# A hybrid decoder layer: state update of the sample sequences in pairs, gate sums on array quarters, a replayed DMA model in the scheduler, Ln and Exp for two roots, and another memory layout

## What is computed

```python
z = a @ w_in                       # q | k | v | r | alow (16 columns) | u | vg
log_a = log_sigmoid(alow @ w_a2 + b_a) / 16     # decay of each key channel
# gated linear attention, token by token:
S = exp(log_a_t) * S + k_t^T v_t ;  o_t = q_t S
o = rmsnorm(o) * silu(r)
m = rmsnorm(gelu(u) * (W_s @ layernorm(gelu(vg)) + b_s))
h = h + concat(o, m) @ w_out ;  h = h + swiglu_ffn(rmsnorm(h))
h = h + rmsnorm(p @ w_ple) * sigmoid(rmsnorm(h) @ w_ple_gate)
```

## Time and profile before

| | |
|---|---|
| median of 3 runs | 1830.63 us (1829.62 to 1832.37) |
| the profiled execution | 1828.47 us |
| its span, slowest core (5) | 1827.2 us |
| spans of the 8 cores | 1819.9 to 1827.2 us |
| mean granted TensorE clock of the cores | 0.991 to 0.996 |
| busy in core 5 | PE 97%, DVE 43%, ACT 29%, POOL 8% |

### The profile page before, as it was taken

One profiled execution on the slowest core, in us unless ns is written; L12 is line 12 of the kernel. 1 busy time (PEld: TensorE's weight loads), 2 busy tenths in 40 slices (PEclk: granted clock), 3 DMA queues, 4 the chain that ended last, 5 costly groups with the idle time before them and its releaser, 6 DMA issues.

```text
span 1827.2 us, 26969 instructions; the slowest of 8 cores (1819.9 to 1827.2 us)
## 1 busy us (share of the span) xinstructions
PE 1774.8 (97%) x10012; PEld 945.1 (52%) x10012; DVE 788.9 (43%) x1232; ACT 522.4 (29%) x932; POOL 142.0 (8%) x139
## 2 busy tenths in 40 slices
PE   4899999999999999999999999999999999999996
PEld 2465545544544566555555555555656565644443
DVE  6565524634533520242424151515151515167886
ACT  4854525655611320000000000000000000017886
POOL 1001212222000000000000000000000000000000
PEclk9899999999999999999999999999999999999998
DMA  9951486065575272424242433334242433376332
GB/s 259 229 128 60 137 199 148 2 116 109 150 145 110 41 127 47 93 47 93 47 84 55 74 66 66 74 57 83 48 90 48 82 58 71 71 146 121 87 100 79
DMA packets 57272, 175.59 MB, mean 96 GB/s; under 512 B 17972, under 2 KB 19380, under 8 KB 53304
## 3 DMA queue, kind: packets, MB, share of 16 engines
q0 software_dynamic: 28960, 108.60, 33.2%
q1 hardware_dynamic: 27896, 64.74, 10.7%
q10 hardware_dynamic: 288, 0.52, 0.1%
HBM read 259.90 MB, written 18.87 MB: 153 GB/s over the span
## 4 chain that ended last, share of the span: by engine, by line
PE 93%; DMA 2%; DVE 2%; ACT 1%; issue 1%; SPq 0%; ACTq 0%; DVEq 0%
PE pf L510 92%; DMA arena<-xp 2%; PE pf L520 2%; ACT arena L472 1%; DVE arena L482 1%; SPq L200 0%; DVE arena L759 0%; DVE arena L490 0%; ACT L472 0%; ACT arena L476 0%; ACT L503 0%; ACTq L200 0%; DVE pf L490 0%; ACT arena L503 0%; DVEq L146 0%
## 5 line engine op out<-in xcount | busy, mean ns | idle before, releaser
L510 PE MATMUL pf<-arena 128*128 128x512 bf16 (+4 forms) x9352 | 1736.2, 350 | 17.4 <-DVE arena L482 3.7
L510 PEld LDWEIGHTS pf<-arena 128*128 128x128 bf16 (+1 forms) x9352 | 902.0, 99 | 835.2 <-issue 34.3
L482 DVE TENSOR_TENSOR arena<-pf,arena 128x512 f32<-128x512 f32 (+3 forms) x657 | 431.4, 661 | 787.4 <-PE pf L510 726.5
L472 ACT ACTIVATE arena<-pf 128x384 bf16<-128x384 f32 (+4 forms) x310 | 160.2, 527 | 978.1 <-PE pf L510 960.8
L472 ACT ACTIVATE arena<-arena 128x512 f32<-128x512 f32 (+8 forms) x124 | 128.2, 1045 | 91.6 <-DVE arena L482 38.1
L490 DVE SCALAR_TENSOR_TENSOR arena<-arena 128x2048 bf16<-128x2048 f32 (+4 forms) x66 | 117.4, 1790 | 12.3 <-DMA arena<-arena 4.3
L200 POOL DMA_DIRECT2D arena<-w_f x55 | 39.0, 710 | 999.9 <-PE pf L510 940.5
L482 DVE TENSOR_TENSOR arena<-arena 128x512 f32<-128x512 f32 (+7 forms) x122 | 91.1, 758 | 55.6 <-ACT arena L472 39.8
L486 POOL TENSOR_TENSOR arena<-arena 128x1024 f32<-128x1024 f32 (+1 forms) x34 | 76.3, 2251 | 266.1 <-ACT arena L476 124.9
L490 DVE SCALAR_TENSOR_TENSOR arena<-pf,arena 128x128 f32<-128x128 f32 (+4 forms) x136 | 54.8, 454 | 45.7 <-PE pf L510 31.8
L476 ACT COPY arena<-pf 128x1024 bf16<-128x1024 bf16 (+2 forms) x51 | 48.9, 969 | 84.1 <-PE pf L520 81.0
(11 more groups left out here) (33 smaller groups left out, 117.5 us busy)
## 6 DMA issues: line engine op xcount, KB each, us to landing
arena<-w_f POOLq DMA_DIRECT2D x44, 1024.0 KB, 9.6
arena<-w_f POOLq DMA_DIRECT2D x11, 2048.0 KB, 14.8
arena<-xm SPq DMA_DIRECT2D x18, 1024.0 KB, 10.5
arena<-w_tok POOLq DMA_DIRECT2D x8, 2048.0 KB, 20.8
arena<-xp SPq DMA_DIRECT2D x8, 1024.0 KB, 18.4
arena<-st SPq DMA_DIRECT2D x16, 512.0 KB, 4.6
sso<-arena SPq DMA_DIRECT2D x16, 512.0 KB, 2.9
arena<-w_out POOLq DMA_DIRECT2D x4, 2048.0 KB, 26.0
```

Source lines behind the costliest of these rows:

```text
L472: S.op("act", lambda: nc.scalar.activation(out=out, in_=in_, func=func, **kw), reads=reads, writes=writes, cost=c_act(n, ptr) + (0.17 if " ...
L482: S.op("dve", lambda: nc.vector.tensor_tensor(out=out, in0=a, in1=b, op=op), reads=reads, writes=writes, cost=c_dve(n, rate))
L510: ins = nc.tensor.matmul(o, lhsT=l, rhs=r, start=st, stop=sp_)
```

## The change

It has six parts.

1. **Gate sums on array quarters.** `walow2` holds the 16 columns once (padded to 32). Product k of 16 goes to the PSUM partitions 32(k mod 4) to 32(k mod 4) + 31, so four products with different data stand side by side in four column strips of the array, and each strip sums a quarter of the products. ACT copies the four partial sums to memory, and one float32 product of 512 columns with the 0/1 matrix `fold` adds them and lays the result four times over the partitions, as before.
2. **Sample pairs.** The 16 sequences are taken as 4j + q. For q = 0 to 3 there is one `qTm[q]` and one masked `ktm[q]` for four sequences (4 masks in place of 16, with the columns of `E4`), and the sequences go in pairs of strips j = (0, 1), (2, 3): the output products have 32 weight columns each and write 32 partitions each, the state products use 32 rows each and write two banks. The number of products stays 128 of 256 columns. Four state buffers in place of three.
3. **Roots by logarithm.** `xnorm_p1` makes 1/sqrt(x) as Exp(-0.5 Ln(x)), both on ACT, with no square root and no reciprocal. Other norms are as before.
4. **The scheduler's DMA model.** The first window is ordered five times; after each, `_landings` replays the loads on both queues with their issue times (each queue in its order, two active queues halve the rate) and the next pass uses the mean of old and new landings.
5. **The own part** is recorded in another order (`own_gen`): the values of tile 0 come ahead of the decay of the first half, and the sample states start 4 steps later.
6. **Memory.** `silur` and `stmp` move up to the region that the decay tiles leave, two `qTm` to the region of `vtok`, and `s0f` grows.

The diff, cut to what is named later:

```diff
     def _order(self, ops, deps):
+        land, start = {}, dict(self.efree)
+        for _ in range(5 if self.model0 else 1):
+            self.efree = dict(start)
+            order, issued = self._pass(ops, deps, land)
+            land = self._landings(ops, issued, land)
...
+    def _landings(self, ops, issued, old):
+
+        qs = {"hw": [], "sw": []}
+        for i, t in issued:
+            o = ops[i]
+            if o.nb >= 7e4:
+                q = "sw" if o.e == "pool" else "hw"
+                qs[q].append([max(t + DMA_LAG[q], DMA_FIRST if self.model0 else 0.0), o.nb, i])
+        land, t = {}, 0.0
+        while qs["hw"] or qs["sw"]:
+            act = [q for q in qs if qs[q] and qs[q][0][0] <= t]
+            nxt = min(qs[q][0][0] for q in qs if qs[q] and q not in act) if any(qs[q] and q not in act for q in qs) else 1e9
+            if not act:
+                t = nxt
+                continue
+            r = 1.03 * DMA_RATE / len(act)
+            dt = min([qs[q][0][1] / r for q in act] + [nxt - t])
+            t += dt
+            for q in act:
+                qs[q][0][1] -= r * dt
+                if qs[q][0][1] < 1.0:
+                    land[qs[q].pop(0)[2]] = t + DMA_END
+        return {i: (v if i not in old else 0.5 * v + 0.5 * old[i]) for i, v in land.items()}
...
-        for c in range(4):
-            S.op("pool", lambda: nc.gpsimd.tensor_copy(out=walow4[:, :, 32 * c:32 * c + 16], in_=walow), reads=[Bwalow], writes=[Bwalow4],
-                 cost=0.8)
+        S.op("pool", lambda: nc.gpsimd.tensor_copy(out=walow2[:, :, 0:16], in_=walow), reads=[Bwalow], writes=[Bwalow2], cost=0.8)
+        fold, r_ = MI.T([128, 4, 32], F32)
+        Bfold = S.buf("fold", r_)
+        S.op("dve", lambda: nc.vector.reduce_sum(out=fold[:, 0, :], in_=identf.rearrange("p (j r) -> p r j", j=4), axis=AX.X),
+             reads=[Bidf], writes=[Bfold], cost=0.3)
+        for c in range(1, 4):
+            DCOPY(fold[:, c, :], fold[:, 0, :], [Bfold], [Bfold], 32)
+        E4, r_ = MI.T([128, 4], F32)
+        BE4 = S.buf("E4", r_)
+        S.op("dve", lambda: nc.vector.reduce_sum(out=E4, in_=ET.rearrange("p (j q) -> p q j", j=4), axis=AX.X), reads=[BET],
...
-            o = bank[:, 0:n].rearrange("p (t j) -> p t j", j=128)
-            dense(o, lambda k: walow4[:, k, :], lambda k: aTv[:, tiles[0]:tiles[-1] + 1, k, :], 16, [Bwalow4] + Brd, [Bb], n)
+            MM([(bank[32 * (k % 4):32 * (k % 4) + 32, 0:n].rearrange("p (t j) -> p t j", j=128), walow2[:, k, :],
+                 aTv[:, tiles[0]:tiles[-1] + 1, k, :], k < 4, k >= 12) for k in range(16)], [Bwalow2] + Brd, [Bb], c_mm(16, n) / 3)
+            ACOPY(alowT[:, 0:n], bank[:, 0:n], [Bb], [Balow], n)
+            bank, Bb = nextpf()
+            MM([(bank[:, 0:n], fold.rearrange("p c r -> p (c r)"), alowT[:, 0:n], True, True)], [Bfold, Balow], [Bb], c_mm(4, n))
             ACT(alowT[:, 0:n], bank[:, 0:n], AF.Identity, [Bb, Bonec], [Balow], n, 1, bias=onec)
             bks = [nextpf() for _ in range(4)]
...
-            RSTD(ss[:, 1:2], ss[:, 0:1], [Bss], [Bss])
+            ACT(ss[:, 1:2], ss[:, 0:1], AF.Ln, [Bss], [Bss], 1, bias=EPS)
+            ACT(ss[:, 1:2], ss[:, 1:2], AF.Exp, [Bss], [Bss], 1, scale=-0.5)
             STT(xn, x_, ss[:, 1:2], gmix, ALU.mult, ALU.mult, [Bx_, Bss] + Bgmix, Bxn, D)
...
-            for i in range(2):
-                dset(qTm[i], BqTm[i], 0.0, 0.3)
-            S.bst = SAMPLE_BOOST
-            for i in range(16):
-                S.bst = SAMPLE_BOOST
-                sl, s3 = i % 2, i % 3
-                S.dma("sp", s0f[s3], st0[i], writes=[Bs0f[s3]])
-                ACOPY(s0b[sl], s0f[s3], [Bs0f[s3]], [Bs0b[sl]], 1024)
-                PTT(s0f[s3], s0f[s3], dsm[:, :, i:i + 1].to_broadcast([128, 4, 256]), ALU.mult, [Bs0f[s3], Bdsm], [Bs0f[s3]], 1024)
-                if i >= 2:
-                    dset(qTm[sl][:, :, 8 * (i - 2):8 * (i - 1)], BqTm[sl], 0.0, 0.15)
-                DCOPY(qTm[sl][:, :, 8 * i:8 * i + 8], qTs[:, :, 8 * i:8 * i + 8], Bq, [BqTm[sl]], 32)
-                ACT(ktm[sl], kt, AF.Copy, Bkt + [BET], [Bktm[sl]], 512, 1, scale=ET[:, i:i + 1])
-                MM([(ob[h // 2][0][:, (h % 2) * 256:(h % 2 + 1) * 256], qTm[sl][:, h, :], s0b[sl][:, h, :], i == 0 and h % 2 == 0,
-                     False) for h in range(4)], [BqTm[sl], Bs0b[sl]], [ob[0][1], ob[1][1]], 0.45)
-                bks = [nextpf(), nextpf()]
-                MM([(bks[h // 2][0][:, (h % 2) * 256:(h % 2 + 1) * 256], ktm[sl][:, h * 128:(h + 1) * 128],
-                     vt[:, h * 256:(h + 1) * 256], True, True) for h in range(4)], [Bktm[sl]] + Bvt, [bks[0][1], bks[1][1]], 0.45)
+            for q in range(4):
+                dset(qTm[q], BqTm[q], 0.0, 0.3)
+                DCOPY(qTm[q].rearrange("p h (j s) -> p h j s", j=4)[:, :, :, 8 * q:8 * q + 8],
+                      qTs.rearrange("p h (j s) -> p h j s", j=4)[:, :, :, 8 * q:8 * q + 8], Bq, [BqTm[q]], 128)
+                ACT(ktm[q], kt, AF.Copy, Bkt + [BE4], [Bktm[q]], 512, 1, scale=E4[:, q:q + 1])
+            for n_ in range(8):
+                q, jp = n_ // 2, n_ % 2
+                jj = (2 * jp, 2 * jp + 1)
+                for x, j in enumerate(jj):
+                    i, s4 = 4 * j + q, j
+                    S.dma("sp", s0f[s4], st0[i], writes=[Bs0f[s4]])
+                    ACOPY(s0b[x], s0f[s4], [Bs0f[s4]], [Bs0b[x]], 1024)
+                    PTT(s0f[s4], s0f[s4], dsm[:, :, i:i + 1].to_broadcast([128, 4, 256]), ALU.mult, [Bs0f[s4], Bdsm], [Bs0f[s4]], 1024)
+                MM([(ob[h // 2][0][32 * j:32 * j + 32, (h % 2) * 256:(h % 2 + 1) * 256], qTm[q][:, h, 32 * j:32 * j + 32],
+                     s0b[x][:, h, :], q == 0 and h % 2 == 0, False) for h in range(4) for x, j in enumerate(jj)],
+                   [BqTm[q]] + Bs0b, [ob[0][1], ob[1][1]], 0.5)
                 for hh in range(2):
-                    TT(s0f[s3][:, 2 * hh:2 * hh + 2, :], bks[hh][0][:].rearrange("p (a v) -> p a v", a=2),
-                       s0f[s3][:, 2 * hh:2 * hh + 2, :], ALU.add, [bks[hh][1], Bs0f[s3]], [Bs0f[s3]], 512)
-                S.dma("sp", sso[i], s0f[s3], reads=[Bs0f[s3]], key=Bs0f[s3])
-                S.bst = 0.0
+                    bks = [nextpf(), nextpf()]
+                    MM([(bks[x][0][:, u * 256:(u + 1) * 256], ktm[q][32 * j:32 * j + 32, (2 * hh + u) * 128:(2 * hh + u + 1) * 128],
+                         vt[32 * j:32 * j + 32, (2 * hh + u) * 256:(2 * hh + u + 1) * 256], True, True)
+                        for u in range(2) for x, j in enumerate(jj)], [Bktm[q]] + Bvt, [bks[0][1], bks[1][1]], 0.25)
+                    for x, j in enumerate(jj):
+                        TT(s0f[j][:, 2 * hh:2 * hh + 2, :], bks[x][0][:].rearrange("p (a v) -> p a v", a=2),
+                           s0f[j][:, 2 * hh:2 * hh + 2, :], ALU.add, [bks[x][1], Bs0f[j]], [Bs0f[j]], 512)
+                    if hh == 0:
+                        yield
+                        yield
+                for x, j in enumerate(jj):
+                    S.dma("sp", sso[4 * j + q], s0f[j], reads=[Bs0f[j]], key=Bs0f[j])
                 yield
                 yield
...
         def own_gen():
+            yield from v_tile(0)
             main_decay(0)
+            for t in (1, 2):
+                yield from v_tile(t)
             yield from main_kq(0)
             main_decay(1)
-            for t in range(VF):
-                yield from v_tile(t)
+            yield from v_tile(3)
             yield from main_kq(1)
-            for t in range(VF, 8):
+            for t in range(4, 8):
                 yield from v_tile(t)
 
         main_decay(2)
         run_streams(main_kq(2))
         run_streams(v_tile(8))
-        run_streams(own_gen(), sample_gen())
+        og = own_gen()
+        for n_ in range(4):
+            next(og)
+        run_streams(og, sample_gen())
...
-        attb, Battb = pair([128, 4, 128], BF16, "attb")
-        on, Bon = pair([128, 1024], BF16, "on")
+        silur, Bsilur = pair([128, 1024], BF16, "silur", 2)
+        stmp, Bstmp = pair([128, 512], F32, "stmp")
         ojunk, r_ = MI.T([128, 256], BF16, "r")
         Bojunk = S.buf("ojunk", r_)
         oss, Boss = pair([128, 8], F32, "oss")
-        stmp, Bstmp = pair([128, 512], F32, "stmp")
-        silur, Bsilur = pair([128, 1024], BF16, "silur", 2)
         Tt, r_ = MI.T([128, 4, 256], F32, "r")
+        attb, Battb = pair([128, 4, 128], BF16, "attb")
+        on, Bon = pair([128, 1024], BF16, "on")
```

66 lines of the change are left out of this document (44 added, 22 removed).

## The result

The change takes 1842.72 us (median of 5 runs) where the kernel before, run beside it, takes 1830.76; the ratio is 1.0063 with a 95% interval of 1.0049 to 1.0077. The prediction was 1815.5 and faster. The profiled execution took 1843.4 us, 1.6 of it outside the span of the slowest core (6). The spans of the cores lie in two groups, 1827.7 to 1829.0 (cores 1, 2, 4) and 1837.3 to 1841.8 (the other five), where those of before lay from 1819.9 to 1827.2.

A forecast was written before the change was run, and what follows sets the result against it. PE, busy 97% of the span, was taken as the bound. Terms -9.0 + 1.0 - 2.9 - 2.2 - 2.0 = -15.1 from 1828.47 gave 1813.4; with 2.2 for the median, 1815.5 us, range 1806 to 1826.

The forecast's parts named there:

- Prices of instructions: On PE: 16 strip products 0.9 us, a fold 1.0, entering and leaving strips 0.2 for a batch.
- strips do not run abreast: Rival, chance 0.10: strip products on PE do not overlap, so gate sums and sample part cost more; 1831.5 us.
- each change of shape is dear: Rival, chance 0.05: switching PE between full width and strips empties the array; at 1 us each, 1838.4 us.
- The first part: -9.0: Before the large product: reordering and roots without table loads start it at 78.6 in place of 87.65, 9.0 us gained.
- Given back in the large product: +1.0: In the large product: more SP loads make the values' weights late, between 0 and 5 us; 1 taken.
- the gain of the start is held by loads: Rival, chance 0.18: later weights eat the start's gain, leaving -2.0 in place of -8.0; 1821.5 us.
- Gate sums in the own part: -2.9: Own part: gate sums on strips save 1.35 us for each of two halves, the sample tile's 0.2.
- Own order: -2.0: Own part: value products around the first decay mostly remove a 2.71 us wait and the slow clock behind; 2.0 us gained.
- Sample states: -2.2: Sample part: pairs abreast take 7.0 us in place of 14.0, less 4.8 for changes of shape; 2.2 us gained.
- The memory layout: nothing: Where PE is full: the new layout lets `r_tile` start earlier, worth nothing.
- a term for a slow clock that goes: Behind the wait before the own keys: the slow 4 us, worth 1.2 us, should mostly go.

The follow-up runs named there:

- later start alone: The kernel before, with the sample stage begun after four own steps and not with the first: ratio 1.0054.
- pairs alone: The kernel before, with the sample states in pairs (masks, strips, four state buffers) and nothing else changed: 1842.84 us, ratio 1.0079.
- pairs paced closer: The kernel before with sample states in pairs, the stage giving way three times for a pair and not four: 1834.52 us, ratio 1.0037.
- the best repaired version: The change, sample stage begun at once and paced closer, g_gout load after the prompt state's store, one more bank step: 1827.87 to 1829.99 us undisturbed.

## Why the prediction was wrong, step by step

**Prices of instructions: right.** PE rows of the change: gate sums of 512 columns (at the lower clock, 29.14), those of 128 columns, a fold, 17-row products.

```profile
29.14 1.90 PE L552 MATMUL pf<-arena 128*32 128x512 bf16 x16 [1.09 <-DVE arena L521]
...
119.88 0.41 PE L552 MATMUL pf<-arena 128*32 128x128 bf16 x16
...
202.84 1.10 PE L552 MATMUL pf<-arena 128*128 128x512 f32 x2 [0.58 <-DVE arena L524]
205.03 1.14 PE L552 MATMUL pf<-arena 17*128 17x512 f32 x8 [1.09 <-ACT arena L514]
```

At full clock 16 strip products took 0.98 us (forecast 0.9), a fold 0.93 (1.0), a pair's output batch 0.55, its state batch 0.32 (forecast 0.44 to 0.7 and 0.22 to 0.45), and the next wide block 0.1 more. Strips run four abreast, and a change of shape costs some 0.1 us. The rivals "strips do not run abreast" and "each change of shape is dear" are out. TensorEngine Tiling (Array Packing) in the Trainium skill, section Key Properties, has TensorE drained at a change of the tiling mode; the trace agrees in kind, with some 0.1 us.

**"The first part: -9.0": a third was never there, a quarter was not reached, the rest was held by a load.** PE and ACT rows of the change:

```profile
52.69 4.59 PE L552 MATMUL pf<-arena 128*128 128x512 bf16 x32 [1.66 <-DMA arena<-w_k]
58.11 1.10 PE L552 MATMUL pf<-arena 128*128 128x512 f32 x2 [0.84 <-ACT arena L518]
...
81.04 13.97 PE L552 MATMUL pf<-arena 128*128 128x512 bf16 x64 [0.80 <-ACT arena L514]
...
97.92 2.34 PE L552 MATMUL pf<-arena 128*128 128x256 bf16 x20 [2.01 <-DMA arena<-w_tok]
```

```profile
42.04 2.04 ACT L514 ACTIVATE arena<-pf 128x512 f32<-128x512 f32 x4
44.17 1.91 ACT L514 ACTIVATE arena<-arena 128x2048 f32<-128x2048 f32 x1
...
65.24 2.04 ACT L514 ACTIVATE arena<-pf 128x512 f32<-128x512 f32 x4
67.37 3.71 ACT L514 ACTIVATE arena<-arena 128x2048 f32<-128x2048 f32 x2
```

The steps up to 67 came as written: the key chunk waits for its weights at 52.7, the second float32 gate products came at 61.9 to 63.0 (62.9 forecast), Ln follows Exp with no table load. Behind the Exps another large activation stood in line (3.71 for two in place of 1.91), and the large product began at 81.0 (78.6 forecast; the terms written there add up to 78.3). But the 87.65 it was compared with came from core 5, the slowest of that run; on the other seven it began at 82.9 to 85.0. So the gain was 3 us on core 6 (84.1 before) and 3.5 in the mean of the eight.

**"Given back in the large product: +1.0": the wrong end of my own range.** I had written that loads could take back 5 us and took 1. The second block of the values' weights landed at 96.0 to 99.1 (94.4 forecast, 89.4 to 91.3 before), PE waited 2.0 us for it on core 6, and the first `s_part` moved from 91.3 to 93.4 (96.4 on core 5) to 96.7 to 99.3. At the sample gate's product the mean of the cores is 122.9, against 124.1 before: 1.2 us gained where 8 were forecast. The rival "the gain of the start is held by loads", which I gave 0.18, is what the first part did. DMA: Bandwidth & Descriptors in the Trainium skill, section Queues, rings and completion order, has each DMA engine take turns between the queues it has work for, packet by packet; by it, more loads waiting on SP must slow POOL's weights. The trace agrees: from 45 to 90 us core 6 moved 6.46 MB on SP's queue and 4.29 on POOL's, before 5.84 and 4.60.

**"Gate sums in the own part: -2.9" and "Own order: -2.0".** The prices held, and the wait of 2.71 us before the own keys went. It came back elsewhere: between 202 and 207, around the second decay, PE idles 0.58, 1.09 and 0.86 (the first two stand above, at 202.84 and 205.03). From 60 to 230 PE idles 8.5 to 11.6 us on the eight cores, where before it idled 8.6 to 9.6. So of the 2.0 us nothing came. That the wait moved to the next link of the same chain is how I read it; no run takes the own order alone.

**"Sample states: -2.2": the step that failed.** The arithmetic of PE was right, and PE was not what bounded that part. I wrote that "if PE did wait there for pairs, its cover are the value products beside them". PE works in its written order: the value products stand behind the waiting batch and cover nothing. And I took "from 200 on it is full" as a property of the work, where it was one of the order: ten states were through before 2 MB weight loads began to share the DMA engines. The loop of a state buffer (store, load, cast, decay, addition) takes about 11 us in quiet (2.9 and 4.6 by the issues of before, and 3.7 for cast, decay and addition) and 30 among the weights, by the chain above. I had costed the later start of the stage ("the sample states start 4 steps later") at nothing. Four kernels show it: later start alone +9 us, pairs alone +15, pairs paced closer +6.5, the change with cut weight loads -12 (of the first three, 1 to 2 us lie in the kernel's last part, in one direction or the other).

**"The memory layout: nothing".** It let a small load overtake a store that ACT waits for: 3 us. **The banks' turn** was in no step: 2 to 3 us.

**The clock.** The sum had a term for a slow clock that goes, and none for one that comes. Between 60 and 420 (1 - clock) x time is 4.9 us more in the change on core 6, on core 0 10.8.

So the sum for the slowest core: by the prices the work fell about as forecast; the start gave 1 to 2 us in place of 8; the states' waits and the clock behind them cost about 12 (by the cut loads), the store 3, the banks 2 to 3; the own order's 2.0 did not come. That is 26 of the 27 us between forecast and result, though the parts overlap. From 1839.5 the states, the store and the banks account for the way down to about 1823, of which the best repaired version (1829) has two thirds: moving the states ahead put waits into 160 to 230, and these I did not get rid of. Two rivals of the prediction were also summed a little wrong, without effect on it: by its own terms the one of strips that do not run abreast comes to +0.2 and not +1, and that of dear changes of shape starts from -20.7 and not -20.2.

## What to carry to other kernels

A stretch in which the bounding engine is full tells nothing of its reserve: before an edit there, find for each buffer loop (store, reload, convert) how long it takes in quiet and under the heaviest load that will share the DMA engines, and how far ahead of its use it is. Work that stands behind a waiting instruction on the same engine is no cover. Read a mark on all cores before taking its distance as a gain, and with a list scheduler take out parts one at a time only while watching the order, since a changed cost reorders everything.

## What was not expected of the hardware

A 0.5 MB state load takes 3.6 us in quiet, and up to 17.6 (issued at 261.5) beside a weight load on the other queue; halving the rate would at most double it. Several transfers on SP's queue stand behind each other there, and the chain above shows them 13 us apiece. How the queues share in detail stays open.

Cores that run the same program split in two groups in the profiled run, 12 us apart; in the other runs other cores are the slow ones, over the same spread but without so clear a gap. In the change core 0 idles 15.0 us from 230 to 310, core 1 5.9; with the weight loads cut both are under 1.1. What tips a core was not found.
